# Attention core on TensorE: two groups of transposes moved ahead of the next stage's scores

## The chip, the cores and the metric

The kernel runs on one core of a Trainium2 chip. The metric is the device time of one execution in microseconds (us), smaller is better. The engines named below are TensorE (PE, with its weight loads PEld), VectorE (DVE), ScalarE (ACT), GpSimd (POOL) and SyncE (SP, which issues transfers).

## The reference

The program computes two blocks on 1024 tokens of width 1024, in float32: an attention layer and a Hyena layer, then a second block with four mixing branches and a feed-forward layer. The change touches only the attention core of the first layer:

```python
s = jnp.einsum("bqhgd,bkhd->bhgqk", _f32(qi), kf) * scale
p = jax.nn.softmax(s, axis=-1)
return jnp.einsum("bhgqk,bkhe->bqhge", p, vf)
```

There are 16 query heads: 8 with 64 features that share 2 key heads (grouped queries), and 8 with 64 + 32 features (latent attention). Queries are the 1024 latent tokens; keys and values are 1280 tokens (1024 latent and 256 of context).

## The kernel before

The order of each engine's work is written out by hand, one Python function per engine and part. The attention core runs 64 stages (`STAGES`). A stage `s` treats one block of 128 query tokens and one pair of heads `e` = 0, 1; eight pairs make a block, the first four (`p < 4`) of the grouped kind, the other four of the latent kind, which need a second set of score products (line 636).

In a stage:

- **Scores** (`scores_pe`, lines 630 and 636): PE writes 128 queries x 1280 keys for each of the two heads into PSUM, tile `attn_aux` for head 0 and `attn_far` for head 1. There is one such pair of tiles, so the scores of stage s + 1 may only be written once both exponentials of stage s have read them (semaphore `exped`).
- **Maximum** (`maximum`, lines 733 and 735): DVE reduces each head's scores to a row maximum and scales it.
- **Softening** (`soften`, line 715): ACT takes the exponential of each head's scores with that maximum as bias, adds up the rows (an instruction that reads the accumulator follows each), and writes `probs` in `attn_work`. `exped` is raised by each head.
- **Turning** (`turn_group_pe`, line 659): PE transposes the probabilities in five groups, 0 to 4, of four 128x128 blocks. Groups go through two PSUM banks of `attn_dense`: groups 0, 2, 3 through bank 0, groups 1 and 4 through bank 1. So a group waits until the one before it in its bank has been copied out (semaphores `copied[0]` and `copied[1]`).
- **Copies** (`copy`): groups 0, 1 and 3 are copied out by ACT (line 707), groups 2 and 4 by DVE (line 740).
- **Weighing** (`weigh_pe`, lines 672 and 676): PE multiplies the values with the turned probabilities, for the stage before; it writes bank 1.
- **Keeping** (`keep`, lines 746 and 748): DVE copies the widened shares out of bank 1, multiplies, and raises `stored`. Group 4 waits for `stored`, since it writes the same bank.

The queues of ACT and DVE for one turn of the loop are, in order: ACT: copy 0, copy 1 of stage s, exponentials of both heads of s + 1, copy 3 of stage s. DVE: reciprocal of the sums (line 754), maxima of both heads of s + 1, copy 2 of s, keep of s - 1, copy 4 of s. The change leaves both queues as they are.

PE executes `core_pe`. A wait of PE holds back all that stands behind it in this queue.

Of the kernel before, what the change touches and what calls it, by code (L numbers as in the profile page):

```python
# [615 lines left out]
def scores_pe(pe, Y, s):  # L616

    tokens, p = stage(s)
    if s:
        pe.wait_ge(Y.exped, 2 * s)  # L620
    else:
        pe.wait_ge(Y.kv_read, 4 + NT)
        pe.wait_ge(Y.va_read, NT)
        pe.wait_ge(Y.roped, len(ROPES))
        Y.dense.done(pe, "u3")
    for lo, hi in segments(N):
        for e in range(2):
            rows = slice(64 * e, 64 * e + 64)
            keys = Y.ka[rows, lo:hi] if p < 4 else Y.km[rows, p - 4, lo:hi]
            mm = pe.matmul(Y.scores[e][:, lo:hi], Y.Q[rows, p, tokens], keys, start=True, stop=(p < 4))  # L630
            if p < 4 and hi == N:
                mm.then_inc(Y.scored, 1)
        if p >= 4:
            for e in range(2):
                rows = slice(64 * e, 64 * e + ROPE)
                mm = pe.matmul(Y.scores[e][:, lo:hi], Y.Q[rows, p + 4, tokens], Y.kpe[rows, lo:hi], start=False, stop=True)  # L636
                if hi == N:
                    mm.then_inc(Y.scored, 1)


def turn_group_pe(pe, Y, s, j):

    bank = Y.banks[j % 2] if j < 3 else Y.banks[(j + 1) % 2]
    if s == 0 and j < 2:
        for b in range(2):
            pe.wait_ge(Y.dense.emptied[b], Y.dense.at["u7"] + 1)
    if s or j >= 2:
        if j in (0, 2, 3):
            pe.wait_ge(Y.copied[0], 3 * s + (0, 0, 1, 2)[j])
        elif j == 1:  # L650
            pe.wait_ge(Y.copied[1], 2 * s)
        else:
            pe.wait_ge(Y.copied[1], 2 * s + 1)
            if s:
                pe.wait_ge(Y.stored, s)
    for e in range(2):
        for kk in range(2):
            n, k = 2 * e + kk, 2 * j + kk
            tr = pe.transpose(bank[:, n * P:(n + 1) * P], Y.probs[:, s % 2, e, k * P:(k + 1) * P], Y.ident)  # L659
    tr.then_inc(Y.turned_up, 1)  # L660


def weigh_pe(pe, Y, s):

    tokens, p = stage(s)
    bank = Y.banks[1]
    pe.wait_ge(Y.copied[1], 2 * (s + 1) + (1 if s + 1 < STAGES else 0))
    pe.wait_ge(Y.copied[0], 3 * (s + 1))
    pe.wait_ge(Y.shared, s + 1)
    for e in range(2):  # L670
        at = 2 * (s % 2) + e
        pe.matmul(bank[64 * e:64 * e + 64, P:2 * P], spread(Y.share[:, at:at + 1], [P, HD]), Y.ident, start=True, stop=True)
    for k in range(NT):
        for e in range(2):
            v = Y.va[:, k, 64 * e:64 * e + 64] if p < 4 else Y.vm[:, k, HD * (2 * (p - 4) + e):HD * (2 * (p - 4) + e + 1)]
            mm = pe.matmul(bank[64 * e:64 * e + 64, 0:P], v, Y.turned[:, s % 2, 4 * (k // 2) + 2 * e + k % 2], start=(k == 0),
                           stop=(k == NT - 1))
    mm.then_inc(Y.weighed, 1)


def core_pe(pe, Y):
    scores_pe(pe, Y, 0)
    for s in range(STAGES):
        pe.wait_ge(Y.exped, 2 * s + 2)
        if s + 1 < STAGES:
            scores_pe(pe, Y, s + 1)
        for j in range(3):
            turn_group_pe(pe, Y, s, j)
        if s:
            weigh_pe(pe, Y, s - 1)  # L690
        for j in (3, 4):
            turn_group_pe(pe, Y, s, j)
    weigh_pe(pe, Y, STAGES - 1)
# [85 lines left out]
def attention_layer(nc, A, x_out, mod, one_plus, K):  # L779
    with Phase(nc, "attn") as ph:  # L780
        Y = Attention(nc, ph, A, mod, one_plus, K)
        with ph.block() as block:
            @block.sync
            def _(sp):
                attention_sp(sp, Y)
                store_rows(sp, Y, x_out)

            @block.tensor
            def _(pe):
                front_pe(pe, Y)  # L790
                core_pe(pe, Y)
                Y.dense.multiply(pe, SEG * 2 * DT)

            @block.scalar
            def _(act):
                front_act(act, Y, A["x"], A["ctx"])
                core_act(act, Y)
                Y.dense.evict(act, SEG * DT)

            @block.vector  # L800
            def _(dve):
                front_dve(dve, Y)
                core_dve(dve, Y)
                back_dve(dve, Y)
# [2365 lines left out]
```

## Time and profile before

| what | value |
|---|---|
| median of 3 runs | 5220.36 us (5216.55 to 5220.53) |
| profiled execution | 5216.07 us |
| its span in the trace | 5214.3 us |
| PE busy | 4836.2 us, 93% |
| DVE busy | 1997.6 us, 38% |
| ACT busy | 988.1 us, 19% |
| attention core, first scores to last keep | 349.7 us to 989.5 us of the span |

Busy shares are averages over all layers; the core is about an eighth of the span. In the timeline views a row is one instruction or several merged ones: start, duration, engine, line, operation, what it writes and reads, count, and in brackets the idle time of the engine before it with what ended that time.

### The profile page before, as it was taken

The page shows a single profiled execution, that of the slowest core. Times are in us where ns is not written, and L with a number is a line of the kernel's source. Part 1 is how long each engine was busy: PE and PEld are TensorE (multiplying, and loading weights), DVE is VectorE, ACT ScalarE, POOL GpSimd, SP SyncE. Part 2 cuts the span into 40 slices and gives each one's busy share as a digit, 9 for nine tenths or more (in the row PEclk, how much of TensorE's full clock was granted, in tenths as well). Part 3 has the DMA queues.
Part 4 walks back from the last instruction along what each step waited for, and adds up shares of the span by engine and source line. Part 5 has one row for each costly group of instructions (what it writes and reads, how often), then busy time and mean ns, then how long its engine had stood idle before and what let it go on. Part 6 is the DMA issues. An engine that isn't in the chain of part 4 may idle for free.

```text
span 5214.3 us, 40015 instructions
## 1 busy us (share of the span) xinstructions
PE 4836.2 (93%) x16966; PEld 2373.9 (46%) x16966; DVE 1997.6 (38%) x2340; ACT 988.1 (19%) x1318; POOL 3.9 (0%) x7
## 2 busy tenths in 40 slices
PE   7989999996999988889888898999999999999998
PEld 3446565542444434344455444444444444444443
DVE  3445555313333366563454544423511124333102
ACT  1134444202111100001333232222200000000000
POOL 0000000000000000000000000000000000000000
PEclk8999999997999999999999999999999999999999
DMA  5100000112232322222000001112221111111211
GB/s 234 60 29 1 1 1 1 45 39 110 89 105 94 140 89 111 93 113 74 33 21 22 25 33 41 37 41 77 83 89 39 36 63 49 41 46 43 72 40 51
DMA packets 85693, 313.95 MB, mean 60 GB/s; under 512 B 9061, under 2 KB 27237, under 8 KB 77450
## 3 DMA queue, kind: packets, MB, share of 16 engines
q1 hardware_dynamic: 68156, 293.57, 15.6%
q10 hardware_dynamic: 17360, 17.83, 1.0%
q8 instruction: 135, 2.21, 0.2%
q14 instruction: 42, 0.34, 0.0%
HBM read 254.22 MB, written 57.15 MB: 60 GB/s over the span
## 4 chain that ended last, share of the span: by engine, by line
PE 64%; DVE 9%; issue 2%; ACT 2%; DMA 0%; DVEq 0%; SPq 0%; ACTq 0%
PE late_dense L115 40%; PE late_four L2787 6%; PE late_two L2787 3%; PE late_four L1023 3%; PE late_four L1241 1%; PE late_four L2022 1%; PE late_two L1320 1%; PE late_two L1312 1%; PE late_four L1040 1%; PE late_four L1035 1%; DVE late_arena L2232 1%; PE late_two L1258 1%; PE late_two L2345 0%; PE late_two L2347 0%; PE late_two L2048 0%
## 5 line engine op out<-in xcount | busy, mean ns | idle before, releaser
L115 PE MATMUL late_dense<-late_arena 128*128 128x512 f32 x5416 | 2378.8, 599 | 24.7 <-DVE late_arena L2705 10.0
L115 PEld LDWEIGHTS late_dense<-late_arena 128*128 128x128 f32 x5416 | 1035.1, 192 | 1313.5 <-issue 1301.8
L128 ACT ACTIVATE late_arena<-late_dense 128x512 f32<-128x512 f32 x226 | 134.8, 597 | 1396.3 <-PE late_dense L115 1383.3
L2787 PE MATMUL late_four<-late_arena 128*128 128x512 f32 x752 | 326.6, 592 | 0.0
L115 PE MATMUL attn_dense<-attn_h,attn_wbuf 128*128 128x512 f32 x576 | 253.3, 598 | 7.6 <-DVE attn_h L551 6.6
L2787 PEld LDWEIGHTS late_four<-late_arena 128*128 128x128 f32 x752 | 142.9, 190 | 179.8 <-issue 176.7
L659 PE MATMUL attn_dense<-matrices,attn_work 128*128 128x128 f32 x1280 | 193.9, 282 | 32.0 <-ACT attn_work L707 15.8
L2705 DVE TENSOR_TENSOR late_arena<-late_dense,late_arena 128x512 f32<-128x512 f32 x64 | 44.2, 691 | 420.1 <-PE late_dense L115 420.1
L2022 PE MATMUL late_four<-late_arena 128*128 128x128 f32 (+1 forms) x1024 | 119.4, 318 | 84.9 <-DVE late_arena L2165 54.5
L1023 PE MATMUL late_four<-late_arena 128*128 128x512 f32 x384 | 171.5, 600 | 9.7 <-DVE late_arena L1057 6.6
L659 PEld LDWEIGHTS attn_dense<-matrices,attn_work 128*128 128x128 f32 x1280 | 135.2, 140 | 92.5 <-issue 58.8
L115 PEld LDWEIGHTS attn_dense<-attn_h,attn_wbuf 128*128 128x128 f32 x576 | 109.6, 191 | 146.5 <-issue 139.6
L733 DVE TENSOR_REDUCE attn_top<-attn_aux 128x1 f32<-128x1280 f32 x64 | 95.5, 1492 | 205.3 <-PE attn_far L636 151.3
L707 ACT ACTIVATE attn_work<-attn_dense 128x512 f32<-128x512 f32 x192 | 107.9, 596 | 329.1 <-PE attn_dense L659 329.1
L2728 DVE TENSOR_TENSOR late_arena<-late_dense,late_arena 128x512 f32<-128x512 f32 x32 | 22.1, 692 | 368.5 <-PE late_dense L115 368.5
L2787 PE MATMUL late_two<-late_arena 128*128 128x512 f32 x368 | 161.7, 592 | 0.0
L2022 PEld LDWEIGHTS late_four<-late_arena 128*128 128x128 f32 (+1 forms) x1024 | 112.4, 227 | 105.1 <-DVE late_arena L2165 57.3
L874 ACT ACTIVATE late_arena<-late_arena 128x512 f32<-128x512 f32 x48 | 30.3, 631 | 552.0 <-DVE late_arena L2728 405.9
L2868 DVE TENSOR_TENSOR late_arena<-late_four,late_arena 128x512 f32<-128x512 f32 x93 | 63.3, 689 | 186.8 <-PE late_four L2787 184.1
L1023 PEld LDWEIGHTS late_four<-late_arena 128*128 128x128 f32 x384 | 72.6, 191 | 101.8 <-issue 86.7
L1241 PE MATMUL late_four<-late_arena 65*128 65x512 f32 x128 | 82.6, 801 | 31.7 <-DVE late_arena L1485 10.5
L115 PE MATMUL attn_dense<-attn_q,attn_wbuf 128*128 128x512 f32 x256 | 110.1, 592 | 2.0 <-issue 2.0
(374 smaller groups left out, 4889.2 us busy)
## 6 DMA issues: line engine op xcount, KB each, us to landing
attn_q<-in_ada_w SPq DMA_DIRECT2D x12, 2048.0 KB, 9.5
late_arena<-in_w_ffn_in SPq DMA_DIRECT2D x44, 512.0 KB, 4.2
late_arena<-in_hy_tables SPq DMA_DIRECT2D x16, 1280.0 KB, 6.1
late_arena<-in_hy_w_in SPq DMA_DIRECT2D x32, 512.0 KB, 3.5
spectrum<-late_arena SPq DMA_DIRECT2D x8, 2048.0 KB, 8.5
late_arena<-spectrum SPq DMA_DIRECT2D x8, 2048.0 KB, 12.5
late_arena<-in_w_gates SPq DMA_DIRECT2D x32, 512.0 KB, 3.4
late_arena<-x SPq DMA_DIRECT2D x6, 2048.0 KB, 10.2
```

What stands on the lines that cost most here:

```text
L115: mm = pe.matmul(self.ps[:, n % SEG], self.wbuf[:, slot, k], job.rhs[:, k, cols], start=(job.first and k == 0), stop=(job.last and k == kt ...
L128: act.activation(job.out[:, cols], self.ps[:, n % SEG], job.func, scale=job.scale, bias=job.bias).then_inc(self.emptied[n % SEG], 1)
L659: tr = pe.transpose(bank[:, n * P:(n + 1) * P], Y.probs[:, s % 2, e, k * P:(k + 1) * P], Y.ident)
L707: act.activation(dst, src, ACT.Copy).then_inc(sem, 1)
L733: dve.reduce_max(Y.top[:, at:at + 1], Y.scores[e][:, 0:N], AX_X).then_inc(Y.topped, 1)
L1023: mm = pe.matmul(Y.group[:, 2 * a + part], Y.table[:, r, part, k], rhs[:, 2 * r + k], start=(k == 0), stop=(k == 1))
L1035: pe.matmul(Y.group[:, part], Y.table[:, r, part, k], rhs[:, 2 * r + k], start=(r == 1 and k == 0), stop=(r == 3 and k == 1))
L1040: mm = pe.matmul(Y.group[:, 2 + part], table[:, part, k], rhs[:, 2 * r + k], start=(r == 1 and k == 0), stop=(r == 3 and k == 1))
L1241: mm = pe.matmul(group[:, 2 * (q % 2) + way], Y.hid[:, q * P:(q + 1) * P], Y.mix[:, way, cols], start=True, stop=True)
L2022: mm = pe.matmul(ps[:, (u + h) % 2, at], left[t.rows[h], at], right[t.rows[h], at], start=True, stop=True)
L2787: mm = pe.matmul(product_bank(M, name, i), left[:, k], right[:, k], start=(k == 0), stop=(k == 3))
L2868: dve.tensor_tensor(out, product_bank(M, product, i), other, ALU.add).then_inc(M.summed_up, 1)
```

## The change

On PE, groups 0 and 1 of stage s are issued ahead of the scores of stage s + 1; group 2 stays behind them.

```diff
     scores_pe(pe, Y, 0)
     for s in range(STAGES):
         pe.wait_ge(Y.exped, 2 * s + 2)
+        turn_group_pe(pe, Y, s, 0)
+        turn_group_pe(pe, Y, s, 1)
         if s + 1 < STAGES:
             scores_pe(pe, Y, s + 1)
-        for j in range(3):
-            turn_group_pe(pe, Y, s, j)
+        turn_group_pe(pe, Y, s, 2)
         if s:
             weigh_pe(pe, Y, s - 1)
         for j in (3, 4):
```

PE's queue before, in one of the early stages of the grouped kind, from the middle of one turn of the loop to the next; a row names the semaphores that its first instruction waits for. The rows are group 3, group 4, the scores of the next stage, then groups 0 and 1:

```order
L659 MATMUL attn_dense<-matrices,attn_work 128x128 [waits attn_copied0]
L659 MATMUL attn_dense<-matrices,attn_work 128x128 x3
L659 MATMUL attn_dense<-matrices,attn_work 128x128 [waits attn_stored,attn_copied1]
L659 MATMUL attn_dense<-matrices,attn_work 128x128 x3
L630 MATMUL attn_aux<-attn_ka,attn_q 128x512 [waits attn_exped]
L630 MATMUL attn_far<-attn_ka,attn_q 128x512
...
L659 MATMUL attn_dense<-matrices,attn_work 128x128 [waits attn_copied0]
L659 MATMUL attn_dense<-matrices,attn_work 128x128 x3
L659 MATMUL attn_dense<-matrices,attn_work 128x128 [waits attn_copied1]
L659 MATMUL attn_dense<-matrices,attn_work 128x128 x3
```

The same place of PE's queue after the change, groups 3, 4, then 0 and 1 of the next stage, then scores:

```order
L659 MATMUL attn_dense<-matrices,attn_work 128x128 [waits attn_copied0]
L659 MATMUL attn_dense<-matrices,attn_work 128x128 x3
L659 MATMUL attn_dense<-matrices,attn_work 128x128 [waits attn_stored,attn_copied1]
L659 MATMUL attn_dense<-matrices,attn_work 128x128 x3
L659 MATMUL attn_dense<-matrices,attn_work 128x128 [waits attn_copied0,attn_exped]
L659 MATMUL attn_dense<-matrices,attn_work 128x128 x3
L659 MATMUL attn_dense<-matrices,attn_work 128x128 [waits attn_copied1]
L659 MATMUL attn_dense<-matrices,attn_work 128x128 x3
L630 MATMUL attn_aux<-attn_ka,attn_q 128x512 [waits attn_exped]
L630 MATMUL attn_far<-attn_ka,attn_q 128x512
```

Group 1's wait for `copied[1]` (the copy of group 4 just issued) and group 0's wait for `copied[0]` (the copy of group 3) now stand ahead of the scores.

At the start of the core, PE's queue differs as follows (stage 0; groups 0 and 1 wait there for the emptied banks of the layer's front part):

```order
+L659 MATMUL attn_dense<-matrices,attn_work 128x128 [waits attn_emptied1,attn_emptied0,attn_exped]
+L659 MATMUL attn_dense<-matrices,attn_work 128x128 x3
+L659 MATMUL attn_dense<-matrices,attn_work 128x128 [waits attn_emptied1,attn_emptied0]
+L659 MATMUL attn_dense<-matrices,attn_work 128x128 x3
 L630 MATMUL attn_aux<-attn_ka,attn_q 128x512 [waits attn_exped]
 L630 MATMUL attn_far<-attn_ka,attn_q 128x512
```

The eight transposes now stand ahead of the scores of stage 1 too. No instruction is added or taken away on any engine.

## Rows read from the trace of the kernel before

**Rows 1.** The page: busy time of PE, its share of the span, instructions.

```profile
PE 4836.2 (93%) x16966; PEld 2373.9 (46%) x16966; DVE 1997.6 (38%) x2340; ACT 988.1 (19%) x1318; POOL 3.9 (0%) x7
```

**Rows 2.** Who waited for whom, 368.27 to 973.38 us: total us, times, longest.

```profile
ACT attn_work L707 <- PE attn_dense L659: 313.4, 122, 6.3
...
PE attn_dense L659 <- ACT attn_work L707: 15.3, 61, 0.3
```

**Rows 3.** Timeline of one stage, all engines, 489 to 496 us.

```profile
489.43 1.09 PE L659 MATMUL attn_dense<-matrices,attn_work 128*128 128x128 f32 x8
489.53 1.49 DVE L733 TENSOR_REDUCE attn_top<-attn_aux 128x1 f32<-128x1280 f32 x1 [4.73 <-PE attn_far L636]
...
490.77 0.66 PE L659 MATMUL attn_dense<-matrices,attn_work 128*128 128x128 f32 x4 [0.25 <-ACT attn_work L707]
...
491.36 0.44 PE L672 MATMUL attn_dense<-matrices,attn_share 128*64 128x128 f32 x4
...
492.64 0.15 DVE L735 TENSOR_SCALAR attn_minus_top<-attn_top 128x1 f32<-128x1 f32 x1
492.71 0.68 DVE L740 COPY attn_work<-attn_dense 128x512 f32<-128x512 f32 x1
...
493.91 0.66 PE L659 MATMUL attn_dense<-matrices,attn_work 128*128 128x128 f32 x4
494.02 0.29 DVE L746 COPY attn_wide_share<-attn_dense 128x128 f32<-128x128 f32 x1 [0.64 <-PE attn_dense L676]
494.05 0.19 ACT L715 ACTIVATION_READ_ACCUMULATOR attn_work<-attn_far,attn_minus_top 128x1 f32 x1
494.35 0.29 DVE L748 TENSOR_TENSOR attn_q<-attn_dense,attn_wide_share 128x128 f32<-128x128 f32 x1
494.60 0.60 ACT L707 ACTIVATE attn_work<-attn_dense 128x512 f32<-128x512 f32 x1 [0.36 <-PE attn_dense L659]
...
494.79 0.63 PE L659 MATMUL attn_dense<-matrices,attn_work 128*128 128x128 f32 x4 [0.22 <-DVE attn_q L748]
...
495.35 0.69 PE L630 MATMUL attn_aux<-attn_km,attn_q 64*128 64x512 f32 x1
...
495.45 0.69 DVE L740 COPY attn_work<-attn_dense 128x512 f32<-128x512 f32 x1 [0.81 <-PE attn_dense L659]
```

**Rows 4.** Timeline of the last stages, 973 to 981 us.

```profile
973.38 1.49 DVE L733 TENSOR_REDUCE attn_top<-attn_aux 128x1 f32<-128x1280 f32 x1 [4.73 <-PE attn_far L636]
...
979.30 0.69 DVE L740 COPY attn_work<-attn_dense 128x512 f32<-128x512 f32 x1 [0.81 <-PE attn_dense L659]
...
980.05 1.12 PE L659 MATMUL attn_dense<-matrices,attn_work 128*128 128x128 f32 x8 [0.22 <-DVE attn_work L740]
```

**Rows 5.** Timeline of the first stages, 357 to 369 us.

```profile
357.05 1.19 PE L630 MATMUL attn_aux<-attn_ka,attn_q 64*128 64x512 f32 x1 [4.89 <-ACT attn_work L715]
...
360.88 1.49 DVE L733 TENSOR_REDUCE attn_top<-attn_aux 128x1 f32<-128x1280 f32 x1 [3.78 <-PE attn_far L630]
...
364.06 0.68 DVE L740 COPY attn_work<-attn_dense 128x512 f32<-128x512 f32 x1
...
364.80 1.09 PE L659 MATMUL attn_dense<-matrices,attn_work 128*128 128x128 f32 x8 [2.01 <-DVE attn_work L740]
...
365.82 0.69 PE L630 MATMUL attn_aux<-attn_ka,attn_q 64*128 64x512 f32 x1
...
368.27 1.49 DVE L733 TENSOR_REDUCE attn_top<-attn_aux 128x1 f32<-128x1280 f32 x1 [1.58 <-PE attn_far L630]
```

**Rows 6.** Windows: stretch; its length; busy us (instructions) of PE, PEld, DVE, ACT, POOL; granted PE clock as a share; DMA share; GB/s.

```profile
357.00:360.00 3.00, 2.95 (x8) 1.53 (x10) 0.10 (x1) 0.00 (x0) 0.00 (x0) 0.52 0.00 0
360.00:366.00 6.00, 3.74 (x28) 2.54 (x28) 3.87 (x6) 4.32 (x7) 0.00 (x0) 1.00 0.01 3
368.27:973.38 605.11, 576.28 (x5021) 362.87 (x5022) 313.46 (x550) 275.76 (x427) 0.00 (x0) 1.00 0.00 1
976.00:982.00 6.00, 5.33 (x66) 4.29 (x64) 3.24 (x8) 3.72 (x7) 0.00 (x0) 1.00 0.00 0
```

## The prediction, made before the changed kernel ran

> **What bounds the kernel now.** I read the page first: PE is busy 93% of the span [rows 1], so a reader should suspect that PE's queue sets the time and ask where it stands idle. Next the windows: over the steady part of the core PE is busy 576.28 of 605.11 us, DVE 313.46, ACT 275.76, no transfers [rows 6]. Then the waits of that stretch: ACT's copies wait 313.4 us for PE's transposes, and the other way round PE waits 15.3 us for ACT's copy, 61 times [rows 2]; the timeline adds a wait of 0.22 a stage for DVE's product [rows 3]. So the core is bound by PE, with two short stalls a stage. Last the timeline of one stage, which gives the order of events and the slack of each. I count from M, the start of the first row maximum, which follows directly on the end of the scores: M = 489.53 [rows 3]. Then, in us after M:
>
> - groups 0 and 1 start at -0.10, group 2 at 1.24 (it waited for ACT's copy of group 0), weighing at 1.83;
> - DVE is busy with two maxima until its copy of group 2 at 3.18 to 3.86, and copies the widened shares at 4.49;
> - group 3 starts at 4.38, long after copy 2, and group 4 at 5.26, after DVE's product at 4.82;
> - the next scores start at 5.82, and only then does DVE copy group 4, from 5.92 to 6.61. The scores hide that copy completely.
>
> A cycle from M to M is 5.82 us and then the scores. The 61 cycles between 368.27 and 973.38 [rows 4, 5] take 605.11 us.
>
> **The change, part by part.** Nothing is added or dropped; what changes is which waits lie on PE's path.
>
> *Taken away.* Group 2 and weighing now follow directly on the scores, and copies 0 and 1 run beside the scores. Group 2 starts at -0.10, weighing 0.59 later (491.36 less 490.77) at 0.49, which is 1.34 earlier than before. The 0.25 us wait for ACT [rows 2, 3] is gone.
>
> *What is late next: DVE.* Weighing done early frees nothing by itself. The widened shares could be copied 2.66 after weighing starts (494.02 less 491.36), at 3.15, but DVE still has its maxima and copy 2 to do until 3.86, which start from M as before. Group 3 waits for copy 2: in stage 0, where PE had nothing to do in between, the copy ended at 364.74 and the group started at 364.80 [rows 5], 0.06 later. So group 3 starts at 3.92, 0.46 earlier than before, not 1.34.
>
> *Keeping and group 4.* Back-to-back work on DVE starts 0.08 before the end of the one before (492.71 against 492.64 + 0.15), so the wide copy starts at 3.78, the product 0.33 later at 4.11, and group 4 0.44 after that (494.79 less 494.35) at 4.55: 0.71 earlier than before. Up to here the change gains.
>
> *The new wait, on the path.* Group 1 of the next stage needs bank 1, which copy 4 must clear. Copy 4 starts 0.66 after group 4 (495.45 less 494.79), at 5.21. Stage 63 has no scores ahead of its groups, so it shows this order today: copy 4 started at 979.30 and group 1 at 980.05 [rows 4], 0.75 later. Group 1 therefore starts at 5.96, and the scores, one group later (495.35 less 494.79 = 0.56), at 6.52. Behind group 1 on PE stand the scores and then all else; DVE's maxima wait for the scores, and the copies and ACT for the maxima, so this is a closed loop: scores, maxima, copy 2, keep, group 4, copy 4, group 1, scores. Nothing else covers it.
>
> *Group 0* waits for both exponentials, done at 4.71 (494.05 + 0.19), and for copy 3. That copy starts when ACT is free, 4.71 at the latest, since group 3 plus 0.69 (494.60 less 493.91) is 4.61; it lasts 0.60, and group 0 starts by 5.37. Its four transposes take about 0.45 (eight in 1.09 less the tail), so it is done by 5.82, 0.14 before group 1 is released. It costs nothing; were it not covered by copy 4, it would set the scores itself.
>
> *The sum.* A cycle becomes 6.52 instead of 5.82 plus the same scores: +0.70, times 61 = +42.7 us. At the start, two groups stand ahead of the scores of stage 1: +1.09 by the duration of such an eight [rows 3]. Stage 0 has no keep, so its scores followed at 365.82 less 360.88 = 4.94 [rows 5]; in the new order group 3 is at 3.92, group 4 at 4.37, copy 4 at 5.03, group 1 at 5.78, scores at 6.34: +1.40. At the end, group 1 of stage 63 stood 6.67 after M [rows 4] and would now stand at 5.96: -0.71. Sum: 42.7 + 1.1 + 1.4 - 0.7 = **+44.5 us**. Against the profiled execution of 5216.07 us that is 5260.6; the median is 4.3 us above this execution, so 5264.9 against the median. I take 5264.
>
> *Bounds of the cycle.* The trace shows no instance of DVE going from copy 2 straight into keep, or of ACT going from the accumulator into copy 3 in steady state. If DVE dispatches each of the three steps 0.05 quicker than I have it, the cycle gains only 0.55: 61 x 0.55 + 1.8 = +35. If ACT needs the 0.36 us of idle seen before its copy [rows 3] after the exponentials as well, copy 3 runs 5.07 to 5.67, group 0 from 5.73, done 6.18, group 1 and the scores 0.22 later: 61 x 0.92 + 1.8 = +58. I take the sum as computed because each of its steps is a distance between rows of the same kind.
>
> **The clock.** PE was granted 1.00 (2.4 GHz) in the whole steady part, and 0.52, close to its lower level of 1.2 GHz, only after it stood idle for 4.89 us [rows 5, 6]. The new idle times are one of about 1 us ahead of group 3 and two or three below 0.5 us. From 360 to 366 us PE did transposes almost alone, with a 2.01 us stall, at 1.00, and from 976 to 982 us the last two turns met likewise at 1.00 [rows 5, 6]. I count nothing for it.
> The Trainium skill (TensorE: Matmul & The Clock Gate, section Part 4: PE-mode transpose) says that transposes do not count as busy time for the clock gate. By that rule the stretch from the end of weighing to the scores, which grows and now holds four groups instead of two, would bring the clock down in each stage; the two windows named speak against it. The rule is one of the rivals below.
>
> **The rivals.**
>
> *A, the stated sum,* a loop through DVE closed by copy 4. +35 to +58. Chance 0.78.
>
> *B, ACT becomes the releaser* by more than the bound above: copies 0 and 1 now run beside the scores' writes to PSUM and may slow, or copy 3 comes later still. From the 0.14 slack on, each 0.1 us late costs 61 x 0.1 = 6 us; half a microsecond gives 44.5 + 61 x 0.36 = +66, 5287. For: copy 3 is pushed right behind the exponentials. Against: in the old order ACT had 0.36 us idle there. Chance 0.09.
>
> *C, the clock falls each stage.* After the long idle time scores of the grouped kind took 3.83 from first product to maximum (357.05 to 360.88), and 2.45 at full clock (365.82 to 368.27) [rows 5]. That adds 1.38 per stage, 61 x 1.38 = 84, so 5349. Chance 0.05, for the windows at 1.00.
>
> *D, faster.* One mechanism: copy 4 is not last, and PE's queue stays the bound. PE alone would need group 2 at -0.10, weighing 0.49, group 3 at 3.04 (493.91 less 491.36 = 2.55 later), then group 4, 0, 1 every 0.45 and scores 0.56 after group 1, at 4.95: 0.87 less than 5.82, 61 x -0.87 = -53, so 5167. It decides at group 1: it would have to be released before 5.26 rather than at 5.96. DVE's chain from M has two maxima of about 1.5 us in it, which nothing shortens; it would need 0.70 to vanish. For: the removed stall is real. Chance 0.04.
>
> *E, no change that can be told:* the loop loses 0.7 less than computed, ends level. It needs the same 0.6 to 0.7 us. Chance 0.04.
>
> **How the numbers follow.** A measurement of this kernel tells about 0.2%, 10 us, from no change. The likeliest case gives 5255 to 5278 with the offset to the median; adding a part of B and the 4 us between runs, the range is 5248 to 5284, which leaves out C, D, E and the far end of B. Slower: A + B + C, rounded to 0.93; same 0.04; faster 0.03.
>
> **What the changed profile would show.** Right: DVE's wait for PE between keep and copy 4 short; PE's line 659 waiting for DVE's line 740 about 120 times (ahead of group 3, about 1 us; ahead of group 1, about 0.2 to 0.5), and no longer for ACT's line 707 ahead of group 2; cycles of 0.7 us more, equal for both kinds of stage; granted clock 1.00. Wrong: the release ahead of the scores shown as ACT (B), clock below 1.00 in the core (C), or group 1 starting as soon as group 0 ends (D).

## The result: 0.86% slower, as forecast, and the profile after

The changed kernel takes 5264.41 us (median of 4 runs, 5263.73 to 5268.63); the kernel before takes 5220.44 in the same comparison. The ratio is 1.0086, 95% interval 1.0069 to 1.0104: slower by more than the noise, and within the range given. Line numbers behind the changed lines are one higher than before, so the copies of DVE are now L741, those of ACT L708, the maximum L734.

The page of the changed kernel, to be read beside [rows 1]:

```profile
span 5263.0 us, 40014 instructions
PE 4853.9 (92%) x16966; PEld 2377.1 (45%) x16966; DVE 1992.1 (38%) x2340; ACT 988.6 (19%) x1318; POOL 3.9 (0%) x7
```

The same 16966 matrix instructions. PE's busy time grew by 17.7 us, 11.0 of them in the 61 steady cycles and 5.3 at the start of the core, of 48.7 us that the span grew by: most of the time went into waits. Who waited for whom over the 61 steady cycles, from the first maximum of stage 2 to that of stage 63 (total us, times, longest), beside [rows 2]:

```profile
ACT attn_work L716 <- DVE attn_minus_top L736: 319.9, 122, 6.6
...
PEld attn_dense L659 <- DVE attn_work L741: 76.3, 122, 1.1
...
PE attn_dense L659 <- DVE attn_work L741: 49.4, 61, 0.8
...
PE attn_dense L659 <- ACT attn_work L708: 11.8, 61, 0.2
```

PE no longer waits for ACT's copy ahead of group 2. It waits for DVE's copies instead, 122 times, which is twice a cycle: once ahead of group 3, once ahead of group 1. The row of PE counts only 61 of them, because the short wait ahead of group 1 disappears under the tail of the transposes in flight; the row of the weight loads (PEld) shows both. The wait for ACT, 0.2 us in each cycle, is that of group 0 for copy 3. It is not on the loop, since group 0's weight loads are issued by M + 5.74 and group 1 is released only at 5.94. A reader who looks only at PE's row misses the wait that closes the loop.

One cycle of the changed kernel, all engines, beside [rows 3] (the timeline from 372.2 to 378.95 us):

```profile
372.26 0.66 PE L659 MATMUL attn_dense<-matrices,attn_work 128*128 128x128 f32 x4
372.37 1.49 DVE L734 TENSOR_REDUCE attn_top<-attn_aux 128x1 f32<-128x1280 f32 x1 [4.54 <-PE attn_far L630]
372.85 0.44 PE L672 MATMUL attn_dense<-matrices,attn_share 128*64 128x128 f32 x4
...
375.55 0.68 DVE L741 COPY attn_work<-attn_dense 128x512 f32<-128x512 f32 x1
...
376.14 0.28 DVE L747 COPY attn_wide_share<-attn_dense 128x128 f32<-128x128 f32 x1
376.29 1.24 PE L659 MATMUL attn_dense<-matrices,attn_work 128*128 128x128 f32 x8 [0.81 <-DVE attn_work L741]
376.46 0.29 DVE L749 TENSOR_TENSOR attn_q<-attn_dense,attn_wide_share 128x128 f32<-128x128 f32 x1
376.89 0.19 ACT L716 ACTIVATION_READ_ACCUMULATOR attn_work<-attn_far,attn_minus_top 128x1 f32 x1
...
377.56 0.69 DVE L741 COPY attn_work<-attn_dense 128x512 f32<-128x512 f32 x1 [0.81 <-PE attn_dense L659]
377.72 1.25 PE L659 MATMUL attn_dense<-matrices,attn_work 128*128 128x128 f32 x8 [0.20 <-ACT attn_work L708]
...
378.90 0.69 PE L630 MATMUL attn_aux<-attn_ka,attn_q 64*128 64x512 f32 x1
```

With M = 372.37 the steps lie at: weighing 0.48 (forecast 0.49), copy 2 at 3.18 to 3.86, group 3 at 3.92 (3.92), wide copy 3.77 (3.78), product 4.09 (4.11), copy 4 at 5.19 (5.21), group 0 at 5.35 (5.37 at the latest), scores at 6.53 (6.52). Group 1 is hidden in the row of eight that starts with group 0; a narrower look at the weight loads alone shows where it starts:

```profile
378.31 0.42 PEld L659 LDWEIGHTS attn_dense<-matrices,attn_work 128*128 128x128 f32 x4 [0.20 <-DVE attn_work L741]
```

That is M + 5.94 (forecast 5.96), released by copy 4. Group 4 is hidden in a row of eight, too: its weight loads start at 376.87, M + 4.50. Before, such loads started 0.04 ahead of group 4's products (494.75 and 494.79), so the forecast of 4.55 for the products is 4.51 for the loads. The cycle grew alike in both kinds of stage: from 8.27 to 8.98 us in the grouped kind, from 11.42 to 12.14 in the latent kind.

Three stretches of both kernels, from windows between first maxima (length; busy us of PE, PEld, DVE, ACT, POOL; granted clock; DMA). The changed kernel, stage 0 to stage 2, then stage 2 to stage 63:

```profile
350.00:372.37 22.37, 14.24 (x53) 8.54 (x54) 7.92 (x13) 8.66 (x13) 0.00 (x0) 0.69 0.00 1
372.37:1020.89 648.52, 587.27 (x5021) 361.83 (x5022) 307.80 (x550) 275.95 (x427) 0.00 (x0) 1.00 0.00 1
```

The kernel before, stage 0 to stage 2 (its steady stretch is in [rows 6]):

```profile
352.18:368.27 16.09, 8.97 (x45) 5.07 (x46) 7.92 (x12) 7.25 (x11) 0.00 (x0) 0.89 0.00 1
```

The account of the span, before against after:

| stretch | before | after | difference | forecast |
|---|---|---|---|---|
| start to first maximum | 352.18 | 350.00 | -2.2 | 0 |
| stage 0 to stage 2 | 16.09 | 22.37 | +6.3 | +2.5 |
| 61 cycles, stage 2 to 63 | 605.11 | 648.52 | +43.4 | +42.7 |
| stage 63 to the first gate product | 16.40 | 15.68 | -0.7 | -0.7 |
| all behind that | 4224.5 | 4226.4 | +1.9 | 0 |
| span | 5214.3 | 5263.0 | +48.7 | +44.5 |

### The profile page after: what moved, and what is told of

Same layout as the page of the kernel before. It is cut to its first block, busy times and chain, and to the rows that moved or that the text cites. A ratio compares the mean times of both kernels' runs of the same rounds, so it can differ in the third digit from the quotient of the medians.

```text
span 5263.0 us, 40014 instructions
## 1 busy us (share of the span) xinstructions
PE 4853.9 (92%) x16966; PEld 2377.1 (45%) x16966; DVE 1992.1 (38%) x2340; ACT 988.6 (19%) x1318; POOL 3.9 (0%) x7
## 4 chain that ended last, share of the span: by engine, by line
PE 63%; DVE 9%; issue 2%; ACT 2%; DMA 0%; DVEq 0%; SPq 0%; ACTq 0%
PE late_dense L115 40%; PE late_four L2788 6%; PE late_two L2788 3%; PE late_four L1024 3%; PE late_four L1242 1%; PE late_four L2023 1%; PE late_two L1321 1%; PE late_two L1313 1%; PE late_four L1041 1%; PE late_four L1036 1%; DVE late_arena L2233 1%; PE late_two L1259 1%; PE late_two L2346 0%; PE late_two L2348 0%; PE late_two L2049 0%
## 5 line engine op out<-in xcount | busy, mean ns | idle before, releaser
L734 DVE TENSOR_REDUCE attn_top<-attn_aux 128x1 f32<-128x1280 f32 x64 | 95.5, 1492 | 298.5 <-PE attn_far L636 197.3
L716 ACT ACTIVATE attn_work<-attn_aux,attn_minus_top 128x1280 f32<-128x1280 f32 x64 | 85.0, 1328 | 324.7 <-DVE attn_minus_top L736 324.7
L708 ACT ACTIVATE attn_work<-attn_dense 128x512 f32<-128x512 f32 x192 | 114.3, 596 | 58.1 <-PE attn_dense L659 56.8
```

The source lines that it names most:

```text
L708: act.activation(dst, src, ACT.Copy).then_inc(sem, 1)
L716: act.activation(Y.probs[:, s % 2, e], Y.scores[e][:, 0:N], ACT.Exp, bias=Y.minus_top[:, at:at + 1], scale=scale, accum_out=Y.total[:, at: ...
L734: dve.reduce_max(Y.top[:, at:at + 1], Y.scores[e][:, 0:N], AX_X).then_inc(Y.topped, 1)
```

## The experiments

In all of them the steady stretch is the one between the first maxima of stages 2 and 63, and a cycle is a 61st of it: 9.920 us before, 10.631 in the changed kernel. Both are means over the two kinds of stage. Medians of a comparison are set against runs of the kernel before in that same comparison.

**One group ahead instead of two.**

```diff
         turn_group_pe(pe, Y, s, 0)
-        turn_group_pe(pe, Y, s, 1)
         if s + 1 < STAGES:
             scores_pe(pe, Y, s + 1)
+        turn_group_pe(pe, Y, s, 1)
```

> Only group 0 goes ahead of the scores, group 1 stays behind them. Theory (the loop is closed by copy 4 ahead of group 1): group 1 behind the scores finds copy 4 done, so the cycle ends on group 0, which waits only for copy 3: scores at about M + 5.9 where the kernel before has 5.82 and the changed one 6.53; time about 5220 to 5232 us. Rival (any transposes ahead of the scores delay them by their own length, and the loss is the two groups' length): half the loss of the changed kernel, about 5242 us.

Measured: 5226.65 us against 5219.8 (ratio 1.0015, interval 1.0005 to 1.0024); steady stretch 610.74 us, +0.09 a cycle. In one stage the maximum starts at 502.64 and the next scores at 508.55, M + 5.91. The theory gave M + 5.9. Of the 0.71 a cycle, 0.62 comes with group 1. It is not the length of the groups that costs: by length, each of the two would cost half of 0.71, which is 0.36.

**DVE copies group 4 twice,** in either order. The first copy goes into a scratch tile that nothing reads; the output is that of the kernel.

```diff
         dst, src, sem = copy_group(Y, s, j)
+        if j == 4:
+            dve.tensor_copy(Y.again[:].rearrange("p (k c) -> p k c", c=P), src)
         dve.tensor_copy(dst, src).then_inc(sem, 1)
```

> The kernel before, with DVE copying group 4 twice (first into a scratch tile): some 0.6 us more DVE work per stage between group 4 and the release of its bank. Theory: before, the scores hide copy 4 completely (it may end as late as the next maximum), so no change: 5220 us. Rival (DVE's total work or the bank's release time matters in either order): plus 61 x 0.6 = 37 us, 5257 us.

> The changed kernel, with DVE copying group 4 twice. Theory: copy 4 is on the loop ahead of group 1, so its 0.6 us come out in full: 61 x 0.6 = 37 us more than the changed kernel, about 5302 us. Rival (the loss comes from group 0's wait for the exponentials and copy 3, so copy 4 is beside the path): at most 0.3 us of it shows, 5264 to 5280 us.

Measured: in the order before, the steady stretch is 605.09 us against 605.11: nothing, to 0.02 us in 61 cycles. Its median, 5224.1 against 5219.8 (1.0009, interval 1.0000 to 1.0018), is 4 us higher for a reason outside the core: the profiled execution was 11.1 us longer in its span than that of the kernel before, and of these 2.9 lie ahead of the first maximum and 8.2 behind that of stage 63. In the changed order the window of the steady stretch reads

```profile
377.44:1062.48 685.04, 589.85 (x5021) 362.24 (x5022) 344.32 (x611) 275.81 (x427) 0.00 (x0) 1.00 0.00 1
```

against 648.52: 36.5 us more, 0.599 a cycle. DVE's busy time rose by 344.32 less 307.80 = 36.5, the same figure, as 0.60 is about what a copy of 0.68 adds when it overlaps its neighbour by 0.08. All of the added copy lies on the path in the new order, none of it in the old one. The median is 5308.73. The timeline shows group 1 released by the second copy:

```profile
506.89 0.69 DVE L743 COPY attn_again<-attn_dense 128x512 f32<-128x512 f32 x1 [0.81 <-PE attn_dense L660]
507.04 0.63 PE L660 MATMUL attn_dense<-matrices,attn_work 128*128 128x128 f32 x4 [0.19 <-ACT attn_work L709]
507.50 0.68 DVE L744 COPY attn_work<-attn_dense 128x512 f32<-128x512 f32 x1
...
508.23 0.66 PE L660 MATMUL attn_dense<-matrices,attn_work 128*128 128x128 f32 x4 [0.56 <-DVE attn_work L744]
```

**Copies 2 and 3 change engines.** ACT copies group 2 ahead of its exponentials, DVE copies group 3 behind keep.

```diff
 # ACT
         copy(s, 1)
+        copy(s, 2)
         if s + 1 < STAGES:
             soften(s + 1)
-        copy(s, 3)
 # DVE
-        copy(s, 2)
         if s:
             keep(s - 1)
+        copy(s, 3)
         copy(s, 4)
```

> The changed kernel, with two copies swapped between engines: ACT copies group 2 (ahead of its exponentials), DVE copies group 3 (behind keep). Theory (group 3 is held by copy 2 behind DVE's maxima, a link of the loop): group 3 starts right after weighing at M + 3.04, group 4 at about 4.03, group 1 at 5.44, scores at about 6.02 instead of 6.53: 61 x 0.5 = 31 us less than the changed kernel, about 5233 us. Rival (only the last link, copy 4 and group 1, matters): within 5 us of the changed kernel, 5264 us.

> The kernel before with the same swap. Theory: PE's queue sets the time there and neither copy is on its path; the exponentials come 0.7 us later but still end ahead of the next scores: no change, 5220 us. Rival (the swap helps or hurts by itself): more than 10 us either way.

Measured: in the changed order 5226.23 us against 5220.63 (1.0015, interval 1.0005 to 1.0024), steady stretch 612.19, which is 36.3 less than in the changed kernel. In the order before, 5221.44 against 5220.63 (1.0002, interval 0.9992 to 1.0011), steady stretch 605.09: nothing. One stage of the first, M = 503.43:

```profile
506.47 0.66 PE L659 MATMUL attn_dense<-matrices,attn_work 128*128 128x128 f32 x4
...
506.62 0.28 DVE L747 COPY attn_wide_share<-attn_dense 128x128 f32<-128x128 f32 x1
...
507.37 0.63 PE L659 MATMUL attn_dense<-matrices,attn_work 128*128 128x128 f32 x4 [0.24 <-DVE attn_q L749]
...
508.03 0.69 DVE L741 COPY attn_work<-attn_dense 128x512 f32<-128x512 f32 x1 [0.17 <-PE attn_dense L659]
```

Group 3 starts at M + 3.04, to the hundredth as expected. Group 4 follows at 3.94 where 4.03 was expected, the weight loads of group 1 at 5.35 (508.78) where 5.44 was, and the scores at 5.94 where 6.02 was; the wide copy, at 3.19, starts 0.08 before the end of the scaled maximum, as back-to-back work of DVE does. So copy 2 behind DVE's maxima is a second link of the loss, and with it opened the order costs 0.12 a cycle instead of 0.71. Two copies changed places here, not one; but copy 3, which now stands on DVE between keep and copy 4, was finished (507.86) before copy 4 could start (508.03), so the 0.60 gained is that of copy 2.

**The start of the core alone.**

> The order of the kernel before, except that in stage 0 alone the two groups go ahead of the scores. To be read in the trace, from the first row maximum of stage 0 to that of stage 2: 16.09 us before, 22.37 us in the changed kernel, of which the order explains 2.5. If the rest is TensorE's clock staying low for longer because these stages' work begins with transposes and a longer idle time, then stage 0 in the new order alone gives 18 to 20 us or so, with a granted clock near 0.5 behind the start, and the cycles from stage 2 on last as before.

> The changed kernel, except that stage 0 keeps the old order. If the start costs what the trace of the changed kernel shows, the stretch from the first maximum of stage 0 to that of stage 2 falls from 22.37 to about 17 to 18 us, and the span with it by 4 to 5 us; if the low clock comes with the program's start whatever the order, the stretch stays above 20.

```diff
+        if s == 0:                     # only stage 0 in the new order
+            for j in range(2):
+                turn_group_pe(pe, Y, s, j)
         if s + 1 < STAGES:
             scores_pe(pe, Y, s + 1)
-        for j in range(3):
+        for j in range(2 if s == 0 else 0, 3):
             turn_group_pe(pe, Y, s, j)
```

Windows, stage 0 to stage 2, of stage 0 alone in the new order:

```profile
349.53:371.24 21.71, 13.58 (x45) 7.40 (x46) 7.92 (x13) 7.47 (x11) 0.00 (x0) 0.69 0.00 1
```

and of all stages but the first:

```profile
354.24:373.41 19.17, 11.71 (x53) 6.70 (x54) 7.92 (x13) 8.44 (x13) 0.00 (x0) 0.82 0.00 1
```

Both are above what was expected (18 to 20, and 17 to 18), since the clock was low in the following stage, too. The steady stretches are 605.06 and 648.54, as in the two kernels. The times were 5220.31 and 5265.96 us, one run each; the second did not fall with the start, since its core began 4.2 us later than that of the changed kernel. The second run shows something more. Its stage 0 is that of the kernel before, with the same stall of 2.00 us ahead of group 3, and PE was granted the full clock up to 368.29. Then came groups 0 and 1 of stage 1, ahead of the scores, and the clock fell:

```profile
362.85:368.29 5.44, 2.84 (x22) 2.16 (x21) 4.10 (x6) 4.41 (x7) 0.00 (x0) 1.00 0.00 0
369.70:372.30 2.60, 2.60 (x7) 1.18 (x8) 0.00 (x0) 0.60 (x1) 0.00 (x0) 0.52 0.00 0
```

Both runs tie the longer start to a lower clock, but not to one cause, so the clock was held up directly.

**Useless products in the idle times of stage 0.** PE multiplies 128x512 blocks into the two free banks; the products are never read, and the output is that of the kernel. `warm_pe` waits until the banks are free, then multiplies 11 blocks the first time and 6 the second.

```diff
     scores_pe(pe, Y, 0)
+    warm_pe(pe, Y, True)
...
         if s:
             weigh_pe(pe, Y, s - 1)
+        else:
+            warm_pe(pe, Y, False)
```

> The changed kernel, with useless products (128x512, written to the two free banks and never read) on TensorE in the two long idle times of stage 0: 11 ahead of the wait for stage 0's exponentials, 6 where stage 0 has no weighing. Theory (the 3.8 us that the start cost beyond the order are the clock at its lower level behind those idle times): granted clock 1.00 in the 24 us from the first maximum, and from it to that of stage 2 about 17.2 us instead of 22.37; the 61 cycles as in the changed kernel, 648.5; in all about 5 us less, 5259 us. Rival (the start is slow for another reason, of the order or of the waits): the stretch stays near 22.

> The kernel before with the same useless products. Theory: the scores of stage 1 are issued at the full clock, so the stretch from the first maximum to that of stage 2 takes 14.7 us instead of 16.09, and the rest is as before: 1.4 us less in all, which the medians cannot tell. Rival: the products delay the scores or the groups, and the stretch gets longer.

> Group 4 inside the scores, with the same useless products at the start. Theory: the 61 cycles at 594.9 us as without them, and the stretch from the first maximum to that of stage 2 falls from 19.21 to about 15 to 16 us: 5206 to 5208 us, below both kernels. Rival: the start is not the clock's, and the time is that of group 4 inside alone, 5210 us.

(The last of these stands on the kernel with group 4 inside the scores, below.) All three missed in the same way. A float32 product of this size shows as two passes (22 rows for 11 products) and takes 0.87 us, not the 0.43 reckoned with, so PE was busy beyond the idle times. The stretches from stage 0 to stage 2 took 23.27, 22.39 and 22.74 us, at a granted clock of 1.00, and the medians were 5270.04 (1.0100, interval 1.0086 to 1.0113), 5223.73 (1.0011, 1.0002 to 1.0020) and 5214.48 (0.9994, 0.9985 to 1.0003). They show that the clock stayed up with PE kept busy, but they cannot say what the low clock had cost. With 5 and 3 products:

```diff
-    for n in range(11 if first else 6):
+    for n in range(5 if first else 3):
```

> As the changed kernel with useless products, but 5 and 3 of them instead of 11 and 6, since each proved to be two passes of 0.43 us (0.87 us a product, 9.7 us for 11), twice what the first of these runs reckoned with. 5 take 4.4 us, which fits the idle time of 4.8 us. Theory (the 3.8 us of the start are the clock's): granted clock 1.00 from the first maximum on and 17.2 us from it to that of stage 2, instead of 22.37. Rival: the stretch stays near 22.

```profile
353.88:370.95 17.07, 15.63 (x69) 7.96 (x70) 7.92 (x12) 8.34 (x13) 0.00 (x0) 1.00 0.00 1
370.95:1019.50 648.55, 587.35 (x5021) 361.82 (x5022) 307.81 (x550) 275.92 (x427) 0.00 (x0) 1.00 0.00 1
```

17.07 us where 17.2 was expected, at the full clock (2.4 GHz). So 22.37 less 17.07 = 5.3 us of the changed kernel's start were the clock at its lower level. Of the kernel before, 1.4 of its 16.09 us were that too, by the scores of stage 1 (3.83 us against 2.45 at the full clock, [rows 5]); this is an estimate, since the kernel before was not run with 5 and 3 products. The difference, 3.9 us, is what the start cost beyond the forecast (3.8). The median, 5262.31, is 2.1 us below that of the changed kernel, less than medians of different comparisons can tell.

**Group 4 inside the scores,** in the order before. This aims at the wait that PE's queue did have before the change: group 4 waiting for DVE's product.

```diff
         if s + 1 < STAGES:
-            scores_pe(pe, Y, s + 1)
+            scores_pe(pe, Y, s + 1, slice(0, 1))
+        if s:
+            turn_group_pe(pe, Y, s - 1, 4)
+        if s + 1 < STAGES:
+            scores_pe(pe, Y, s + 1, slice(1, 3))
...
-        for j in (3, 4):
-            turn_group_pe(pe, Y, s, j)
+        turn_group_pe(pe, Y, s, 3)
```

> The order of the kernel before, but group 4 of a stage is issued inside the scores of the second next stage, behind their first segment. Theory (PE's path counts, with the waits on it): the wait of group 4 for DVE's product, 0.45 us a stage, is covered by the first segment, and copy 4 still ends before group 1 needs it: scores start at about M + 4.95 plus 0.45 for the group inside, 0.3 to 0.4 less per cycle than 5.82: 5196 to 5203 us. Rival (the wait only moves, since the scores now wait for the second exponential, done at M + 4.71 plus dispatch, or group 1 waits for copy 4): 5215 to 5225 us.

Measured: 5210.55 us against 5219.8 (0.9983, interval 0.9974 to 0.9992): faster than both kernels, but by about half of what was expected: 9 us where 17 to 24 were. The steady stretch is 594.90, -0.167 a cycle where -0.3 to -0.4 was expected. That is 10.2 us, of which the start takes 3.1 back: stage 0 to stage 2 took 19.21 us at a granted clock of 0.73. The timeline of a stage of the grouped kind, whose maximum started at 502.39:

```profile
507.35 0.69 PE L631 MATMUL attn_aux<-attn_ka,attn_q 64*128 64x512 f32 x1
...
508.41 0.66 PE L660 MATMUL attn_dense<-matrices,attn_work 128*128 128x128 f32 x4
509.00 0.69 PE L631 MATMUL attn_aux<-attn_ka,attn_q 64*128 64x512 f32 x1
```

The scores start at M + 4.96, as expected (4.95). The size that was off is the group inside: it takes 0.59 (508.41 to 509.00) and not 0.45. In grouped stages the cut costs a further 0.20: that cycle is 8.20 us, which is 4.96, then the scores' uncut 2.45, then 0.59, and 0.20 remain. In latent stages, whose cycle is 11.15, nothing remains. So a grouped cycle gains 0.07 and a latent one 0.27.

## Why the prediction was right, step by step

**The loop and its size.** The step on which all rested was that the new order closes a loop scores, maxima, copy 2, keep, group 4, copy 4, group 1, scores, in place of a queue of PE with two small stalls. Each link of the loop came out within 0.02 us of its forecast, and the cycle at +0.71 where +0.70 was forecast. That it is a loop, and not only a coincidence of lengths, the experiments show: 0.60 us added to copy 4 lengthens the cycle by 0.60, and by 0.00 in the old order; taking copy 2 from behind the maxima shortens it by 0.60, and by 0.00 in the old order; moving group 1 back behind the scores gives back 0.62.

**What was taken away** was right, too: group 2 and weighing start as forecast, and as forecast the 1.34 us that weighing gains shrink to 0.46 at group 3, and group 1 turns the gain into a loss.

**Group 0** costs nothing in the changed kernel, but only since copy 4 is later: with group 1 out of the way, group 0's wait is the end of a cycle of +0.09. Two small errors met there: copy 3 starts at 4.62, not 4.71, since ACT begins it 0.09 before the read of the accumulator ends (as it did in stage 0 of the kernel before, at 365.50 behind a read from 365.41 to 365.60), and group 0 starts 0.14 after that copy's end, where 0.06 was taken from a copy of DVE.

**The start was mis-sized.** Its two terms, +1.09 and +1.40, measured +2.44 (first maximum to the next: 11.14 against 8.70) and +3.84 (11.23 against 7.39). The prediction counted nothing for the clock, because two windows of the kernel before showed 1.00. At the start PE has stood idle for 4.8 us and comes back at the low clock, which it did before, too; but before, it came back with scores, and the clock rose within them. In the changed kernel it comes back with eight transposes and then the scores, at a granted clock of 0.52 from 354.77 to 361.04, the start and the end of both. The rows that follow an idle time:

```profile
354.77 1.97 PE L659 MATMUL attn_dense<-matrices,attn_work 128*128 128x128 f32 x8 [4.80 <-ACT attn_work L716]
...
365.06 3.87 PE L659 MATMUL attn_dense<-matrices,attn_work 128*128 128x128 f32 x16 [3.36 <-DVE attn_work L741]
```

Between them group 2 ran at the full pace (four in 0.66 us). The second row is four groups at a granted clock of 0.50, behind an idle time of 3.36 us that was 2.01 before, and the first half of the scores of stage 2 is slow as well. The granted clock of the stretch was 0.69 against 0.89, and with the idle times filled it was 1.00 and the stretch 17.07. The prediction's own sum gives 16.09 + 2.5, less the 1.4 that the low clock cost the kernel before: 17.2. So the sum of the order was right, and the term that was missing is the clock's, 3.8 us.

What exactly keeps the clock down is not settled. Neither window held what the new order puts there. Stage 0 has no weighing, so between the scores of stages 1 and 2 PE has only transposes and waits. In the kernel before these took 5.03 us (360.79 to 365.82) with a stall of 2.01, and the clock stayed at 1.00. With all stages but the first in the new order they took 6.91 us, with the same stall and one of 0.34, and it fell, though it had been at its full level. With stage 0 alone in the new order they took 5.92 us with 3.36 idle at a stretch, and it fell. With the copies swapped they took 5.90 us with idle times of 0.69 and 2.44, and it stayed up; that start, which began with the same eight transposes, took 19.44 at 0.82. So both a longer idle time and more transposes ahead of the scores go with the lower clock, in one trace each.

**The agreement of the total is in part luck.** The forecast for the profiled execution was 5260.6 and it took 5264.78; the start cost 3.8 more, the part ahead of the core 2.2 less, the part behind it 1.9 more, the 61 cycles 0.7 more. The medians differ by 44.0 us, the two profiled executions by 48.7: the 4.3 us by which the prediction raised its figure to the median had no counterpart in the changed kernel, whose profiled execution lies within 0.4 us of its median. By chance this stood in for the 3.8 that was missing at the start. The first maximum falls between 347 and 355 us from kernel to kernel, with no edit ahead of it; the cause of that was not looked for.

**The rivals.** B (ACT releases): ACT's copy 3 started right with the end of the exponentials, and group 0 was done before group 1 was released. C (the clock falls in each stage): 1.00 over all 648.52 us, though in each cycle the 3.4 us from the end of weighing (M + 3.10) to the scores hold only transposes and waits; it does fall at the start. By the rule of the Trainium skill (TensorE: Matmul & The Clock Gate, Part 4: PE-mode transpose), that transposes don't count as busy for the clock gate in the way that products do, the steady part should have lost its clock, as the prediction read the rule, and this trace disagrees; the start is compatible with the rule, without showing it. D and E needed DVE's chain to be 0.6 us or more shorter; no link of it moved by more than 0.02. (The chances of A, B and C add up to 0.92, and D alone has 0.04, where the prediction's last sums say 0.93 and 0.03.)

## What to carry to other kernels

Work that is moved ahead of a long operation brings its waits along: ask which copy had been hiding behind that operation, and whether it still ends in time. When the order of a queue changes, write out the new chain link by link from distances between rows of the same kind, from one fixed event to its return; double one suspected link in both orders to see whether it is on the path. Look apart at the first stage, where a link is missing and the engine comes from an idle time. A wait that a product's row does not show can stand in the row of its weight load.

## What the runs showed of the hardware that was not expected

Cutting a run of score products (64 rows of the array, two heads at once) with full-size transposes costs more than the transposes: in grouped stages 0.79 us for a group of four, against the 0.45 reckoned with. The pitch between pairs of score products is 0.43 us within a run, but 0.53 for the first pair after other work: in the same kernel 507.35 to 507.89 behind transposes, and again 509.00 to 509.53. The last pair ahead of the transposes is followed after 0.52 (507.89 to 508.41). These two tenths are the 0.20 that grouped stages lose. Latent stages have such steps in any order, between the products of lines 630 and 636 (in the kernel before 496.40 to 496.94, then 497.46), and lose nothing more.

A float32 product of 128x512 shows as two rows and takes 0.87 us at the full clock (22 rows in 9.71 us, with the tail of the last), although its row gives a mean of about 0.6 us for one pass.
